# Down projection over pairs of token tiles: seven block products for eight, outputs kept in another basis

## The reference, cut to what matters

```python
D_MODEL = 1024
D_FF = 4 * D_MODEL
    x = x + mixed @ w_out
    h2 = rms_norm(x, ln2)
    x = x + jnp.square(jax.nn.relu(h2 @ w_up)) @ w_down
```

## Time and profile before

| | us |
|---|---|
| median of 3 runs | 1531.0 (1529.4 to 1531.0) |
| the profiled execution | 1526.9 |
| its span, from the first to the last thing in the trace | 1525.2 |
| TensorE busy in it | 1423.7 |
| VectorE, ScalarE, GpSimd busy | 735.3, 421.4, 83.2 |

### The profile page before, as it was taken

One profiled execution on the slowest core, in us unless ns is written; L12 is line 12 of the kernel. 1 busy time (PEld: TensorE's weight loads), 2 busy tenths in 40 slices (PEclk: granted clock), 3 DMA queues, 4 the chain that ended last, 5 costly groups with the idle time before them and its releaser, 6 DMA issues.

```text
span 1525.2 us, 19242 instructions
## 1 busy us (share of the span) xinstructions
PE 1423.7 (93%) x7499; PEld 1232.9 (81%) x7499; DVE 735.3 (48%) x1186; ACT 421.4 (28%) x741; POOL 83.2 (5%) x119
## 2 busy tenths in 40 slices
PE   4979989899898993998999999999999999999997
PEld 3765967859677882887989998999889988999896
DVE  6355364453634646675444454444444444444444
ACT  5124233242334546231312211221112211221110
POOL 2510101101000000000000000000000000000000
PEclk8989999999999996999999999999999999999999
DMA  6023432514222112111111110111011110111004
GB/s 186 8 69 91 127 79 68 143 44 120 65 75 68 30 57 94 60 42 47 60 32 55 41 41 28 55 55 41 19 50 55 41 41 28 55 41 44 24 28 125
DMA packets 133130, 92.87 MB, mean 61 GB/s; under 512 B 22358, under 2 KB 122710, under 8 KB 133076
## 3 DMA queue, kind: packets, MB, share of 16 engines
q1 hardware_dynamic: 133076, 92.14, 21.2%
HBM read 78.24 MB, written 9.68 MB: 58 GB/s over the span
## 4 chain that ended last, share of the span: by engine, by line
PE 88%; DVE 6%; ACT 2%; issue 1%; DMA 1%; POOL 1%; SPq 1%; ACTq 0%; DVEq 0%
PE psum L1473 25%; PE psum L1474 25%; PE psum L1475 25%; PE psum L1694 4%; PE psum L1678 1%; PE psum L1650 1%; DVE tops L1207 1%; PE psum L1681 1%; PE psum L1539 1%; PE psum L1772 1%; POOL rs L694 1%; PE psum L1586 1%; PE psum L1561 1%; DVE cross_qk L1199 0%; PE psum L1793 0%
## 5 line engine op out<-in xcount | busy, mean ns | idle before, releaser
L1441 DVE TENSOR_TENSOR mix<-psum,mix 128x512 f32<-128x512 f32 x288 | 196.4, 690 | 160.4 <-PE psum L1475 160.3
L1473 PE MATMUL psum<-h_hi,wu_hi 128*128 128x384 f32 x768 | 258.9, 337 | 4.2 <-DVE mix L1395 4.2
L1474 PE MATMUL psum<-h_lo,wu_hi 128*128 128x384 f32 x768 | 258.6, 337 | 0.0
L1475 PE MATMUL psum<-h_hi,wu_lo 128*128 128x384 f32 x768 | 258.6, 337 | 0.0
L1473 PE MATMUL psum<-wd_hi,u_hi 128*128 128x512 f32 x576 | 224.2, 389 | 3.6 <-issue 3.6
L1474 PE MATMUL psum<-wd_lo,u_hi 128*128 128x512 f32 x576 | 224.1, 389 | 0.0
L1475 PE MATMUL psum<-wd_hi,u_lo 128*128 128x512 f32 x576 | 224.1, 389 | 0.0
L1473 PEld LDWEIGHTS psum<-h_hi,wu_hi 128*128 128x128 f32 x768 | 144.9, 189 | 4.9 <-issue 4.4
L1474 PEld LDWEIGHTS psum<-h_lo,wu_hi 128*128 128x128 f32 x768 | 144.8, 189 | 0.5
L1475 PEld LDWEIGHTS psum<-h_hi,wu_lo 128*128 128x128 f32 x768 | 144.8, 189 | 0.0
L985 ACT CAST wd_hi<-raw 128x1024 fp32r<-128x1024 f32 x32 | 32.1, 1049 | 401.3 <-PE psum L1475 399.9
(11 more groups left out here) (257 smaller groups left out, 2137.3 us busy)
## 6 DMA issues: line engine op xcount, KB each, us to landing
raw<-in_w_up_dram SPq DMA_DIRECT2D x32, 512.0 KB, 4.6
raw<-in_w_down_dram SPq DMA_DIRECT2D x32, 512.0 KB, 3.3
k_c<-in_cache_k_dram SPq DMA_DIRECT2D x32, 256.0 KB, 3.0
raw<-in_w_in_dram SPq DMA_DIRECT2D x32, 192.0 KB, 4.1
out_dram<-mix SPq DMA_DIRECT2D x9, 512.0 KB
x_in<-in_x_prompt_dram SPq DMA_DIRECT2D x8, 512.0 KB, 4.0
v_c<-in_cache_v_dram SPq DMA_DIRECT2D x16, 256.0 KB, 4.9
kts<-in_cache_v_dram SPq DMA_DIRECT2D x16, 256.0 KB, 3.8
```

What stands on the lines that cost most here:

```text
L1441: nc.vector.tensor_tensor(at, psum[:, 4 + 2 * (t % 2) + half, :].rearrange("p (k n) -> p k n", n=P), at, ALU.add).then_inc(y_added, 1)
L1473: nc.tensor.matmul(out, hi(k), r_hi(k), start=first and k == 0, stop=False)
L1474: nc.tensor.matmul(out, hi(k), r_lo(k), start=False, stop=False)
L1475: last = nc.tensor.matmul(out, lo(k), r_hi(k), start=False, stop=end and k == n - 1)
```

## The change

**Pairs.** Eight of the nine token tiles are taken in pairs, (0, 3), (1, 4), (2, 5) and (6, 7). For a pair and a hidden block, the down projection is a product of 2 x 2 blocks: A11 and A12 are the first tile's u in chunks 0 and 1, A21 and A22 the second's; B11, B12 are chunk 0 of w_down in the two halves of the output columns, B21, B22 chunk 1. In place of 8 block products 7 are made, each of 3 matmuls of 512 columns, of combinations of A (S1 to S4, formed in `up`) and of B (T1 to T4, formed in `raw`): A11 B11, S1 T1, A12 B21, S2 T2, S4 B22, S3 T3, A22 T4. The ninth tile has its 12 matmuls as before.

**Outputs in another basis.** `mix` keeps, for three of a pair's four quarters, not the output but differences: `part` subtracts once before the MLP (8 subtractions of 512 columns), each product is added to or subtracted from one or two quarters (10 for a pair, 4 for the ninth tile, 44 a block for 18), and `join` adds back after the last block (8). Five banks of PSUM take the products in turn, three the up units.

**Order.** The up units of the next block stand in pieces of 9, 9 and 6 matmuls between the products of this block; the sixth unit stands whole behind the last product. The last block has no up units. A combination is named by its letter in capitals (S2, T4); GpSimd's own operations are named a22, b22, a21, b11, b21, a11, a12 after the slot that they overwrite: a22 makes S1, b22 T2, a21 S3, b11 T3, b21 T4, a11 S2 and a12 S4.

**GpSimd** forms the combinations: `combine_early` for the first three pairs (384 columns of u at once, and the weights' of 512), `combine_late` for the pair (6, 7), with that pair's and the ninth tile's low parts, and the low part of the second chunk of w_up. ScalarE now also rounds u. The two kinds of weights have slots of `raw` of their own, so that they no longer take turns.

```diff
-    u_hi = sb(mlp, "u_hi", [P, 2, 2, T_ALL], F32R)
-    u_lo = sb(mlp, "u_lo", [P, 2, 2, T_ALL], F32R)
+    u1_hi = sb(mlp, "u1_hi", [P, 7, GN], F32R)
+    u1_lo = sb(mlp, "u1_lo", [P, 7, GN], F32R)
...
+    U_A11, U_A12, U_A22, U_S2, U_S4, U_S3, U_S1 = range(7)
+    W_B11, W_T1, W_B21, W_B22, W_T2, W_T3, W_T4 = range(7)
...
+            def combine_early(b):
+                a11, a12, a21, a22 = up[:, 0, :], up[:, 1, :], up[:, 2, :], up[:, 3, :]
+                b11, b21, first, b22 = raw[:, 2, 0:SPAN], raw[:, 3, 0:SPAN], raw[:, 2, SPAN:], raw[:, 3, SPAN:]
+                pool.wait_ge(u_ready, 4 * b + 2)
+                combined(nc.gpsimd.tensor_tensor(a22, a21, a22, ALU.add), u_combined, 8 * b + 1)
+                pool.wait_ge(wd_ready, 7 * b + 4)
+                combined(nc.gpsimd.tensor_tensor(b22, b22, first, ALU.subtract), wd_combined, 4 * b + 2)
+                combined(nc.gpsimd.tensor_tensor(a21, a11, a21, ALU.subtract), u_combined, 8 * b + 2)
+                combined(nc.gpsimd.tensor_tensor(b11, b22, b11, ALU.subtract), wd_combined, 4 * b + 3)
+                combined(nc.gpsimd.tensor_tensor(b21, b21, b22, ALU.subtract), wd_combined, 4 * b + 4)
+                combined(nc.gpsimd.tensor_tensor(a11, a22, a11, ALU.subtract), u_combined, 8 * b + 3)
+                combined(nc.gpsimd.tensor_tensor(a12, a12, a11, ALU.subtract), u_combined, 8 * b + 4)
...
+            with pool.Fori(0, NFB - 1) as b:
+                up_lo(b + 1)
+                combine_late(b)
+                t1(b + 1)
+                combine_early(b + 1)
...
+            def block_act(b, more):
+                late_units(b)
+                up_hi(b + 1, 1)
+                late_rounded(b)
+                early_units(b + 1)
+                early_rounded(b + 1, PRODUCTS * b)
+                if more:
+                    up_hi(b + 2, 0)
...
+            def block_adds(b, follows, more):
+                add_a11(b, 0)
+                add_s1(b, 0)
+                early_s24(b)
+                add_a12(b, 0)
...
+                add_s2(b, 3)
+                add_s4(b, 3)
+                if follows:
+                    early_a22(b + 1)
+                    down_lo(b + 1, W_B22, raw[:, 3, SPAN:], 4)
+                add_s3(b, 3)
+                add_a22(b, 3)
+                if follows:
+                    down_lo(b + 1, W_T2, raw[:, 3, SPAN:], 5)
+                    early_s31(b + 1)
+                    down_lo(b + 1, W_T3, raw[:, 2, 0:SPAN], 6)
+                    down_lo(b + 1, W_T4, raw[:, 3, 0:SPAN], 7)
+                else:
+                    join(3)
+                if more:
+                    up_lo(b + 2)
...
+            def product(bank, u_hi, u_lo, w, first, end):
+                nc.tensor.matmul(psum[:, bank, :], u_hi, wd_hi[:, w, :], start=first, stop=False)
+                nc.tensor.matmul(psum[:, bank, :], u_hi, wd_lo[:, w, :], start=False, stop=False)
+                return nc.tensor.matmul(psum[:, bank, :], u_lo, wd_hi[:, w, :], start=False, stop=end)
...
+            def block_down(b, ups):
+                for q in range(3):
+                    pair_with(b, q, q, ups)
+                tile8_first(b)
+                if ups:
+                    up_part(b + 1, 3, 0, 3)
+                tile8_last(b)
+                do_a11(b, 3)
+                if ups:
+                    up_part(b + 1, 3, 3, 6)
+                do_s1(b, 3)
+                do_a12(b, 3)
+                if ups:
+                    up_part(b + 1, 3, 6, KC)
+                do_s2(b, 3)
+                do_s4(b, 3)
+                if ups:
+                    up_part(b + 1, 4, 0, 3)
+                do_s3(b, 3)
+                if ups:
+                    up_part(b + 1, 4, 3, 6)
+                do_a22(b, 3)
+                if ups:
+                    up_part(b + 1, 4, 6, KC)
+                    up_part(b + 1, 5, 0, KC)
```

More of the change, by code:

```diff
@@ L593, in up_weights, with down_weights @@
                              ).then_inc(raw_in[c], 16)
[L595 to L597 removed]
+            def down_weights(b):
+                for k in range(2):
+                    sp.dma_start(raw[:, 2 + k, :], w_down[0, bass.ds(b * FB + k * P, P), :]).then_inc(raw_in[2 + k], 16)
             load_xe(0)
@@ L1449, in mlp_dve @@
-            def mlp_dve(i, par, more):
-                for k in range(2):
-                    down_lo(k, V_MLP + 4 * i + 4 + k)
-                for m in range(6):
-                    split_u(i + 1, par, m)
-                    if more and m in (2, 5):
-                        up_lo(m // 3, V_MLP + 4 * i + 6 + m // 3)
-                add_y(i)
-            before = d.n
-            with dve.Fori(0, (MLP_STEPS - 1) // 2) as j:
-                d.enter(j, 12, before)
-                for o in range(2):
-                    mlp_dve(2 * j + o, (o + 1) % 2, True)
-                d.leave(12, before, (MLP_STEPS - 1) // 2)
@@ new lines, in add_s4, with add_s3, add_a22, part @@
+            def add_s4(b, q):
+                add(b, PAIR_AT[q] + 4, PAIR_TILES[q][0], 1)
+            def add_s3(b, q):
+                t1, t2 = PAIR_TILES[q]
+                add(b, PAIR_AT[q] + 5, t2, 1, own=adds_of(PAIR_AT[q]) + 6)
+                add(b, PAIR_AT[q] + 5, t1, 1, ALU.subtract, additions=1, own=adds_of(PAIR_AT[q]) + 7)
+            def add_a22(b, q):
+                add(b, PAIR_AT[q] + 6, PAIR_TILES[q][1], 0)
+            def part(q):
+                t1, t2 = PAIR_TILES[q]
+                for t, half in ((t1, 1), (t2, 0)):
+                    nc.vector.tensor_tensor(half_of(t, half), half_of(t, half), half_of(t2, 1), ALU.subtract).then_inc(x1_parted, 1)
@@ new lines, in _ @@
+            for q in range(4):
+                part(q)
+            dve.wait_ge(x1_parted, 8)
+            early_a1(0)
+            down_lo(0, W_B11, raw[:, 2, 0:SPAN], 1)
+            down_lo(0, W_T1, raw[:, 2, SPAN:], 2)
+            down_lo(0, W_B21, raw[:, 3, 0:SPAN], 3)
+            early_a22(0)
+            down_lo(0, W_B22, raw[:, 3, SPAN:], 4)
+            down_lo(0, W_T2, raw[:, 3, SPAN:], 5)
+            early_s31(0)
+            down_lo(0, W_T3, raw[:, 2, 0:SPAN], 6)
+            down_lo(0, W_T4, raw[:, 3, 0:SPAN], 7)
@@ L1469, in _ @@
+            up_lo(1)
+            with dve.Fori(0, NFB - 2) as b:
+                block_adds(b, True, True)
+            block_adds(NFB - 2, True, False)
+            block_adds(NFB - 1, False, False)
         @block.tensor
@@ L1855, in _ @@
-            mlp_down(NFB - 1, (NFB - 1) % 2, V_MLP + 4 * (NFB - 1) + 4)
+            first_unit(0)
+            turn_h2(NT - 1)
+            first_unit(1)
+            pe.wait_ge(x1_ready, 2 * NT)
+            for m in range(2, 6):
+                first_unit(m)
+            with pe.Fori(0, NFB - 1) as b:
+                block_down(b, True)
+            block_down(NFB - 1, False)
     ctx.close()
```

441 lines of the change are left out of this document (317 added, 124 removed).

## The result

The changed kernel takes 1569.56 us (median of four, 1567.63 to 1570.74) where the kernel before takes 1531.01 (1529.44 to 1531.59): the ratio is 1.0252, 95% interval 1.0234 to 1.027, so it is slower by 2.5%. The prediction was 1559, in a range of 1512 to 1582, with 0.63 on slower; the time is 2.6 us above the forecast's own range of 1549 to 1567. The profiled execution has a span of 1565.9, to stand beside the 1525.2 of before.

A forecast was written before the change was run, and what follows sets the result against it. TensorE alone was taken to bound the MLP stretch; with the change's stalls, 750.4 + 52.7 + 14 × 50.7 + 35.0 + 5.7 = 1553.6 us of span, 1559 after adding the profiled run's difference to the median; range 1512 to 1582.

The forecast's parts named there:

- the forecast's own range: Whole execution: steady blocks of 50.0 to 51.2 us, giving 1549 to 1567 us; chance 0.43.
- The chain's times: Fourth up unit's end through GpSimd's combinations to the up weights' low part: ready at 14.7 us, wanted by TensorE at 12.40.
- the line through the earlier trace: GpSimd two-input operations: 2.14 ns a column and 0.18 us fixed, so 1.0, 1.28 and 2.4 us for 384, 512, 1024 columns.
- Reading together: GpSimd operations and VectorE low parts, both reading SBUF: one waits for the other's end, 0.3 to 0.6 us for GpSimd's combinations.
- The rival without it: Steady blocks with no price for GpSimd and VectorE reading SBUF together: 48.0 us a block, 1518 in all; chance 0.20.
- The early end: Where GpSimd and VectorE wait for each other: either lets go 0.1 to 0.2 us before its end, block 50.0.
- Both stalls: TensorE waits each block: 2.3 us before the first up matmul, 1.6 before S2's product.
- the restart: TensorE after each stall: the next matmul starts late, costing 0.1 us more, twice a block.
- 46.72: TensorE's own work in a steady block, in us, after removing 12 matmuls of 0.2267 (2.72 us).
- The ends: Outside steady blocks: down products from 750.4, first block 2 us more stall, last block 34.5 to 35, tail 5.7.
- The clock's rival: TensorE's clock falls in each block's stalls: 15 × 1.5 = 22 us more, 1581 in all; chance 0.05.
- a block of 48.8: Steady block length, in us, at which the execution would be level with the kernel before.

The follow-up runs named there:

- the one with 48.69: Against the kernel with the second half of w_up's low part on VectorE: b22, b11 and b21 formed by GpSimd again; 1523.60 us, ratio 0.9964.
- S24's low part first: Against the change: VectorE makes the low part of S2 and S4 ahead of the four adds of A11's and S1's products; 1562.12 us, ratio 1.0208.
- b's and S24: Against the change: VectorE forms b22, b11, b21 and makes the low part of S2 and S4 ahead of the four adds; 1536.17 us.
- second half on VectorE: Against the kernel with four edits (b's on VectorE, two low parts earlier, joins on GpSimd): w_up's second-chunk low part on VectorE; 1496.96 us, ratio 0.9788.

## The prediction against the runs, point by point

- **The chain's times were right.** From the end of the fourth unit: a22 was foreseen at 3.3 and starts at 3.30; a12's end at 13.6, it is 13.77; the up weights' low part at 14.7, it is 14.85; TensorE wants it at 12.40, it is 12.42. GpSimd's durations from the line through the earlier trace rows were 1.0, 1.28 and 2.4 for 384, 512 and 1024 columns; the operations that meet nothing take 1.02, 1.30 and 2.37. The waits of a22, b11, b21, a11 and a12 for a low part were foreseen at 0.36, 0.3, 0.6, 0.3 and 0.3, and are 0.39, 0.32, 0.60, 0.32 and 0.30.
- **Reading together was the right mechanism,** out of two single rows. The rival without it would have needed low parts of 0.69; they average 0.97, and with the reading taken out, 0.69. The adds, with one input in PSUM, are free of it as foreseen: 683 ns on the mean in the change. The early end that the prediction allowed for (0.1 to 0.2 us, with a block of 50.0) is there, at 0.13, but the block of 50.0 is not.
- **Both stalls were foreseen** at 2.3 and 1.6; they are 2.42 and 1.58. The steady block is 51.35 for 50.7, 0.15 above the forecast's range. The term that was mis-sized most is the restart, "0.1 each" from the earlier trace rows. The idle time in brackets counts from a matmul's modelled end, 0.39 after its start; the next start without a stall is 0.23 after it. A stall of 2.42 in a row thus puts the next start back by 1424.71 − 1421.90 − 0.23 = 2.58, and 0.11 more is lost at the matmul behind it; likewise 1.74 + 0.07. That is 4.50 where I had 4.1. Of the rest, 0.12 is that I took 50.7 of a sum of 50.8, and 0.13 that TensorE's own row is 46.85 and not 46.72 (46.85 + 4.50 = 51.35). Over fourteen blocks the 0.65 makes 9.1 us, most of the miss.
- **How the two stalls hang together was not seen.** I worked the second out behind the first, and the sum came out right; but nothing in the text says that S24's operand is the later one, at 4.2, so that mending the first alone gains nothing. The run with the up weights moved showed it.
- **The ends.** The down products start at 751.34 for 750.4. The same part of the program ends up to 3 us apart in these kernels (GpSimd's first operation at 744.65 to 747.88), so I put nothing down to it. The first block has 2 us more than the steady one, as foreseen, and so takes 53.3 for 52.7. The last block takes 36.7 for 34.5 to 35:

```profile
1524.07 1.23 DVE L1583 TENSOR_TENSOR wd_lo<-raw,wd_hi 128x512 fp32r<-128x512 f32 x1 [0.19 <-ACT wd_hi L1082]
...
1529.62 0.69 DVE L1612 TENSOR_TENSOR mix<-mix,psum 128x512 f32<-128x512 f32 x1 [0.46 <-PE psum L2115]
1530.88 0.69 DVE L1612 TENSOR_TENSOR mix<-mix,psum 128x512 f32<-128x512 f32 x1 [0.57 <-PE psum L2115]
1532.16 1.88 DVE L1612 TENSOR_TENSOR mix<-mix,psum 128x512 f32<-128x512 f32 x3 [0.59 <-PE psum L2115]
...
1558.84 1.29 DVE L1653 TENSOR_TENSOR mix<-mix 128x512 f32<-128x512 f32 x2
```

  T4's low part ends at 1525.30, 1.8 after the start of TensorE's first product, where I had the first add at 0.9, and three adds then wait for products, as TensorE itself had waited for S24. The tail from 1560.13 is 5.8 for 5.7.
- **The clock's rival** had the right event and the wrong bill. It fell after the first stall in nine of fourteen blocks, 1.6 us each, near the 1.5 taken from the earlier trace rows, and the execution didn't grow, since the second stall covered it. I had added it to the block; beside a wait that ends at a time set by other engines, a slower TensorE costs nothing.
- **The sum.** 0.9 at the start, 0.6 in the first block, 9.1 in the steady ones, 1.7 in the last, 0.1 in the tail: 12.4 on the 1553.6, which is the span of 1565.9. The point from which the sign is decided, a block of 48.8, held to some 3 us of the execution: the run with reading taken out has 48.66 and a span 1.1 above before's, the one with 48.69 (and shorter ends) 2.6 below.

## What to carry to other kernels

Before giving idle GpSimd work that reads SBUF, list what VectorE does meanwhile with both inputs in SBUF, and put one behind the other: here this took 2.7 us of a block in which 2.72 were to be gained. When a row of TensorE waits for several operands, count how late each is if the others weren't, and mend the latest first; and put what an engine can already do (a low part with its input there) ahead of what it will have to do anyway (adds with free banks behind them). Taking away a stall can uncover another cost that lay inside it, so a fix is judged with all of them away.

## What the runs showed of the hardware that I had not expected

- TensorE's granted clock after a stall isn't a matter of the stall's length alone: after 2.42 us idle it fell in nine blocks in a row of the change and in none of the last five, and in thirteen of fourteen with S24's low part first, with the same instructions around; after 1.85 in ten of fourteen; after 1.61, and after 1.17 followed by 0.64, in none. Where it fell, it cost 1.6 us at one stall, and 2.8 at one of 4.8.
- A long operation on GpSimd holds a short one on VectorE for nearly its whole length: 3.14 us for 0.95, beside one of 1024 columns (b's and S24); and it is itself slower, 3.29 for 2.37. The other way, a GpSimd operation of 128 columns took 1269 ns on the mean for 463 where VectorE made 1024 columns of low part (second half on VectorE).
- GpSimd's fills left VectorE's two-input operations alone (687 ns on the mean, where 683 is the mean with GpSimd's combinations cut to 8 columns).
